# Multiplying the second block's weight pages as whole float32 instead of as high and low halves

## What is computed

```python
xn = rmsnorm(h, norm1_g)
proj = xn @ w_in                                   # 1024 -> 3584
q_a, k_a, v_a, q_r, f_r, i_r, g_r = split(proj)
attn = moba_attention(q_a, k_a, v_a)
rec = hgrn2(q_r, f_r, i_r, g_r)
h = h + concatenate([attn, rec]) @ w_out           # 1024 -> 1024
hn = rmsnorm(h, norm2_g)
h = h + peer(hn, peer_wq, peer_subkeys, peer_u, peer_v)
out = rmsnorm(h, normf_g)
```

## Time and profile before

| | us |
|---|---|
| median of three runs | 1626.68 |
| the profiled execution, its own time | 1631.37 |
| its span in the trace | 1629.6 |
| TensorE busy | 1366.6 (84%) |
| VectorE busy | 919.0 (56%) |
| ScalarE busy | 619.4 (38%) |
| GpSimd busy | 546.0 (34%) |
| start of the first of the 24 split pages of the change | about 749 |
| first expert gather | 928.76 |

### The profile page before, as it was taken

One profiled execution on the slowest core, in us unless ns is written; L12 is line 12 of the kernel. 1 busy time (PEld: TensorE's weight loads), 2 busy tenths in 40 slices (PEclk: granted clock), 3 DMA queues, 4 the chain that ended last, 5 costly groups with the idle time before them and its releaser, 6 DMA issues.

```text
span 1629.6 us, 19201 instructions
## 1 busy us (share of the span) xinstructions
PE 1366.6 (84%) x7122; PEld 994.5 (61%) x7122; DVE 919.0 (56%) x1853; ACT 619.4 (38%) x1425; POOL 546.0 (34%) x370
## 2 busy tenths in 40 slices
PE   6978959976966999999999988888777777777786
PEld 5867848955866999999878954444322322223332
DVE  2231896515353578834663646666666666666654
ACT  2002312214342566655445444334444444444443
POOL 0000000000045588887104423343443444444341
PEclk9998978968998999999999999999898889899899
DMA  5443310001334365565325499999999999999997
GB/s 200 155 130 104 104 52 1 1 0 65 104 111 135 104 190 185 181 194 166 95 79 180 166 398 389 378 387 377 396 399 404 408 406 399 400 397 402 408 403 301
DMA packets 67641, 381.03 MB, mean 234 GB/s; under 512 B 7520, under 2 KB 7648, under 8 KB 34400
## 3 DMA queue, kind: packets, MB, share of 16 engines
q0 software_dynamic: 36864, 268.45, 40.7%
q1 hardware_dynamic: 29808, 107.49, 20.6%
q10 hardware_dynamic: 880, 3.93, 0.6%
HBM read 378.79 MB, written 1.05 MB: 233 GB/s over the span
## 4 chain that ended last, share of the span: by engine, by line
PE 59%; DVE 19%; DMA 14%; ACT 4%; issue 3%; POOL 1%; DVEq 0%; SPq 0%; ACTq 0%; POOLq 0%
PE bank L397 23%; PE bank L850 15%; DMA arena_block<-in_experts,arena_block 14%; PE bank L413 4%; PE bank L425 2%; DVE arena_mix L1347 2%; PE bank L529 1%; PE bank L537 1%; PE bank L802 1%; DVE late L1828 1%; PE bank L669 1%; PE bank L535 1%; POOL arena_block L1878 1%; PE bank L395 1%; PE bank L436 1%
## 5 line engine op out<-in xcount | busy, mean ns | idle before, releaser
L850 PE MATMUL bank<-arena_block 128*128 128x512 f32 x1024 | 497.9, 638 | 140.5 <-ACT arena_block L1238 140.3
L1868 POOL TENSOR_TENSOR w_lo<-ring,w_hi 128x1024 fp32r<-128x1024 f32 x110 | 269.3, 2464 | 642.5 <-ACT w_hi L906 642.4
L850 PEld LDWEIGHTS bank<-arena_block 128*128 128x128 f32 x1024 | 201.1, 204 | 428.9 <-ACT arena_block L1238 221.6
L1828 DVE SCALAR_TENSOR_TENSOR late<-arena_block 128x1024 f32<-128x1024 f32 x256 | 307.2, 1223 | 233.0 <-DMA arena_block<-in_experts,arena_block 233.0
L1878 POOL DMA_INDIRECT arena_block<-in_experts,arena_block x256 | 276.5, 1080 | 415.3 <-PE bank L850 384.5
L1232 ACT ACTIVATE arena_block<-arena_block 128x1 f32<-128x1 f32 x256 | 51.6, 202 | 291.6 <-DVE late L1828 289.6
L906 ACT ACTIVATE w_hi<-ring 128x1024 fp32r<-128x1024 f32 x110 | 115.5, 1053 | 99.8 <-PE bank L425 37.3
L397 PE MATMUL bank<-h_norm,ring 128*128 128x256 f32 x576 | 128.3, 381 | 3.1 <-ACT arena_mix L919 3.1
L397 PEld LDWEIGHTS bank<-h_norm,ring 128*128 128x128 f32 x576 | 108.2, 190 | 20.3 <-issue 6.0
L397 PE MATMUL bank<-arena_mix,ring 128*128 128x256 f32 x480 | 107.3, 387 | 13.2 <-DMA ring<-in_pages 13.2
L397 PE MATMUL bank<-x_hi,w_hi 128*128 128x256 f32 x416 | 118.3, 284 | 0.0
(11 more groups left out here) (399 smaller groups left out, 2152.9 us busy)
## 6 DMA issues: line engine op xcount, KB each, us to landing
ring<-in_pages SPq DMA_DIRECT2D x192, 512.0 KB, 3.5
late<-in_pages SPq DMA_DIRECT2D x8, 512.0 KB
arena_block<-in_experts,arena_block POOLq DMA_INDIRECT x256, 12.5
const<-in_const ACTq DMA_DIRECT2D x1, 1136.0 KB, 9.1
x_res<-in_xT SPq DMA_DIRECT2D x2, 512.0 KB, 6.7
arena_mix<-in_memT ACTq DMA_DIRECT2D x1, 1024.0 KB, 12.8
arena_block<-in_subkT ACTq DMA_DIRECT2D x1, 1024.0 KB, 4.9
out_tok<-arena_block SPq DMA_DIRECT2D x4, 256.0 KB, 5.1
```

The lines of the kernel that those rows point to most:

```text
L850: last = mm(bank[2 * tt + j][:, :], diag[:, slot, :], uv[slot][:, D + j * 512:D + (j + 1) * 512], start=False, stop=stop)
L1828: stt(junk[r % 2], uv[s][:, 0:D], 1.0, htok[:, tt, :], ALU.mult, ALU.mult, accum_out=e_act[:, s:s + 1])\
L1868: nc.gpsimd.tensor_tensor(w_lo[:, slot, :], ring[:, slot, :], w_hi[:, slot, :].bitcast(F32), ALU.subtract)\
```

## The change

All pages from in2 on become whole. The 24 split pages are multiplied as float32 from the ring with `hn`, or with `cat` itself for out2. With them go their `w_hi` and `w_lo`, the `x_hi` and `x_lo` of the two norms of the second layer, and `cat_hi` and `cat_lo`. The ring slots of these pages now come free when TensorE has done the page. The waits of TensorE on split inputs become waits on `hn` and on `cat`.

```diff
-WHOLE = list(range(PAGE0["qk"], PAGE0["out2"])) + list(range(PLAIN0, N_PAGES))
+WHOLE = list(range(PAGE0["in2"], N_PAGES))
...
-        linear("in2", x_hi, x_lo, part=(0, 1), ready=("x_split", KT))
+        linear("in2", hn, part=(0, 1), ready=lambda k: (S("x_hn"), k + 1))
...
-            ways = [(hn, ring)] if page in WHOLE else [(x_hi, w_hi), (x_lo, w_hi), (x_hi, w_lo)]
             for k in range(KT):
-                for n_, (y, w) in enumerate(ways):
-                    last = mm(bank_of(stage, i)[:, 0:2 * P], y[:, k, tt * P:(tt + 1) * P], w[:, slot:slot + 2, k * P:(k + 1) * P],
-                              start=k == 0 and n_ == 0, stop=k == KT - 1 and n_ == len(ways) - 1)
+                last = mm(bank_of(stage, i)[:, 0:2 * P], hn[:, k, tt * P:(tt + 1) * P], ring[:, slot:slot + 2, k * P:(k + 1) * P],
+                          start=k == 0, stop=k == KT - 1)
...
-        linear("out2", cat_hi, cat_lo, ready=("cat_split", 0))
+        linear("out2", cat, ready=lambda k: (S("att_oc"), MH + 2 * k + 2) if k < 4 else (S("cat_rec"), k - 3))
...
-            if page < PLAIN0 + SLOTS:
-                ways = products(page, x_hi, x_lo)
-            else:
-                ways = [(late[:, page - PLAIN0 - SLOTS, :], hn)]
+            w = ring[:, page % SLOTS, :] if page < PLAIN0 + SLOTS else late[:, page - PLAIN0 - SLOTS, :]
...
-            A_(x_hi[:, k, :], x[:, k, :], ACT.Identity, scale=V(gain, k)).then_inc(S("x_hi"), 1)
             if i >= 3:
-                A_(hn[:, k, :], x[:, k, :], ACT.Identity, scale=V(gain, k))
+                A_(hn[:, k, :], x[:, k, :], ACT.Identity, scale=V(gain, k)).then_inc(S("x_hn"), 1)
+            else:
+                A_(x_hi[:, k, :], x[:, k, :], ACT.Identity, scale=V(gain, k)).then_inc(S("x_hi"), 1)
...
-            if h % 2:
-                act.wait_ge(S("att_oc"), MH + h + 1)
-                cat_high(ft)
...
-            norm_low(i, j, gain)
+            if i == 2:
+                norm_low(i, j, gain)
...
-            if h:
-                cat_low(3 + h)
-        cat_low(7)
```

More of the change, by code:

```diff
@@ L243, in build @@
     mg_hi, mg_lo = typed(YS_AT, ("mg_hi", "mg_lo"), KT)
-    cat_hi, cat_lo = typed(TYPED0 + 9216, ("cat_hi", "cat_lo"), KT)
     ff_space = [nc.sbuf_tensor(n, [P, FT, T], F32R) for n in ("ff_hi", "ff_lo")]
@@ L375, in products @@
             if page not in NTH:
-                return [(ring[:, slot, :], hn if page in WHOLE else hi)]
+                return [(ring[:, slot, :], hi)]
             return [(w_hi[:, slot, :], hi), (w_hi[:, slot, :], lo), (w_lo[:, slot, :], hi)]
@@ L389, in linear @@
                         if ready and b == 0:
-                            pe.wait_ge(S(ready[0]), ready[1] + k + 1)
+                            pe.wait_ge(*ready(k))
                         for n_, (w, y) in enumerate(ways):
@@ L451, in head_sum @@
             last.then_inc(S("head_sum"), 1)
-        linear("in_a", xg, part=(0, 1), ready=("xg_ready", 0))
+        linear("in_a", xg, part=(0, 1), ready=lambda k: (S("xg_ready"), k + 1))
         pe.wait_ge(S("const_in"), 16)
@@ L645, in _ @@
         linear("out", mg_hi, mg_lo)
-        linear("up", x_hi, x_lo, part=(0, 1), ready=("x_split", 0))
+        linear("up", x_hi, x_lo, part=(0, 1), ready=lambda k: (S("x_split"), k + 1))
         norm_sum(2)
@@ L649, in _ @@
         down()
-        linear("in2", x_hi, x_lo, part=(0, 1), ready=("x_split", KT))
+        linear("in2", hn, part=(0, 1), ready=lambda k: (S("x_hn"), k + 1))
         norm_sum(3)
-        linear("in2", x_hi, x_lo, part=(1, N_IN2 - 1))
+        linear("in2", hn, part=(1, N_IN2 - 1))
         pe.wait_ge(S("norm_inv"), 4)
@@ L660, in by_token @@
             page, tt = PAGE0[stage] + i - i % 2, i % 2
-            if page in WHOLE:
-                page_ready(page)
+            page_ready(page)
             page_ready(page + 1)
@@ L737, in _ @@
             if u < N_QK:
-                linear("qk", x_hi, x_lo, part=(u, 1))
+                linear("qk", hn, part=(u, 1))
             elif u < N_QK + N_TI:
@@ L741, in _ @@
             else:
-                linear("g2", x_hi, x_lo, part=(u - N_QK - N_TI, 1))
+                linear("g2", hn, part=(u - N_QK - N_TI, 1))
             if u == 0:
@@ L793, in query @@
                 pe.wait_ge(S("wq_out"), b - 1)
-            if page < PLAIN0 + SLOTS:
-                ways = products(page, x_hi, x_lo)
-            else:
-                ways = [(late[:, page - PLAIN0 - SLOTS, :], hn)]
+            w = ring[:, page % SLOTS, :] if page < PLAIN0 + SLOTS else late[:, page - PLAIN0 - SLOTS, :]
             for k in range(KT):
                 if b == 0:
[L800 to L803, removed]
+                    pe.wait_ge(S("x_hn"), KT + k + 1)
+                last = mm(bank[4 + b % 2][:, 0:T], w[:, k * P:(k + 1) * P], hn[:, k, :], start=k == 0, stop=k == KT - 1)
             last.then_inc(S("page_done"), 1)
@@ L1080, in _ @@
                 norm_tile(3, "down", j, "norm1_g_2")
-        high_ahead(PAGE0["in2"])
         norm_root(3)
         for b in range(1, N_IN2):
-            high_ahead(PAGE0["in2"] + b)
             if b == 4:
@@ L1127, in mb_done @@
             A_(cat[o:o + 64, ft, :], bank[6 + h % 2][o:o + 64, 0:T], ACT.Copy).then_inc(S("att_oc"), 1)
-            if h % 2:
-                act.wait_ge(S("att_oc"), MH + h + 1)
-                cat_high(ft)
-        def cat_high(k):
-            A_(cat_hi[:, k, :], cat[:, k, :], ACT.Copy).then_inc(S("cat_hi"), 1)
         take_rtok(0, 5)
         act.wait_ge(S("rtok_in"), 1)
-        high_ahead(PAGE0["tv"])
         act.wait_ge(S("in2_out"), N_IN2)
@@ L1197, in _ @@
                 A_(hg_in, hg_in, ACT.Silu).then_inc(S("h_act"), 1)
-        for h in range(GH):
-            act.wait_ge(S("cat_rec"), h + 1)
-            cat_high(4 + h)
         for j in range(KT):
-            high_ahead(PAGE0["out2"] + j)
             if j:
@@ L1683, in mb_share @@
             ts(p_[:, P:3 * P], p_[:, P:3 * P], r_[:, 1:2], None, ALU.mult).then_inc(S("att_p"), 1)
-        def cat_low(k):
-            dve.wait_ge(S("cat_hi"), k + 1)
-            tt_(cat_lo[:, k, :], cat[:, k, :], cat_hi[:, k, :].bitcast(F32), ALU.subtract).then_inc(S("cat_split"), 1)
         for b in range(4):
```

7 lines of the change are left out of this document (removed).

## The result

| | before | after |
|---|---|---|
| median, 11 runs each, on one chip | 1628.68 us | 1637.15 us |
| lowest and highest | 1625.85, 1633.5 | 1635.02, 1640.11 |
| ratio | | 1.0050 (95%: 1.0038 to 1.0062) |

The change makes the kernel slower by 0.5%, some 8.5 us (6.2 to 10.1 by the interval). The profiled execution took 1640.11 us, the longest of the eleven.

The account below looks back on a forecast made before the run. TensorE was taken to bound the kernel up to the first expert gather, transfers from there on. 10.7 us to head 0's scores, -0.85 for the clock and +2.5 for late pages gave 12.3 us: 1639.0 us, range 1634.5 to 1643.

Parts of the forecast that it names:

- The price of a page: On TensorE, a whole page takes 3.46 us against 2.88 split, 0.58 us more; 24 pages make 13.9 us.
- the four passes of the Trainium skill: Rival: a whole page costs four passes at the split price, 3.84 us, 9 us above the sum; chance 0.01.
- in2 and tv: Twelve pages turned whole cost 7.0 us, less stalls of 0.23 and 0.34 us that go: +6.4 us.
- qk to g2: Pages already whole, with no one on the chain waiting for the removed copies and subtractions: 0, bounds -0.5 to +0.5.
- The ring: Page slots are held until TensorE is through, yet loads land in time: 0, upper bound about 2 us at one place.
- out2 and its clock: Out2 pages +3.4 us; the low clock behind the idle time costs 0 or -1.7, half taken: -0.85.
- Queries 0 and 1: First two query pages: +0.35 us for query 0, 0.58 for query 1 with its clock loss kept; +0.9 us.
- The late pages: Loads issued near the first gather come later and move the fourth dot product and the end: +2.5 us, bounds 0 and 3.5.
- The ScalarE wait of 11.4 us: Expert stage's start; rival of failed feeding lets it grow or ring loads come late: 3 to 8 us more, chance 0.07.
- The signs of being wrong: Wrong if a stretch without changed pages changes its length by over 1 us, or TensorE waits for a ring load.
- the 938 to 940: Time in us at which the first expert gather was expected to start in the changed kernel.
- The rival "absorbed": Expert stage's seams take in 2 us or more of delay, leaving +3.3 to +7.8 us, 1630 to 1634.5; chance 0.07.

Follow-up runs that it names:

- e_out2wq: Out2 and the first four query pages whole, in2 and tv split as in the kernel before; 1.0040 of before.
- e_all_early: The changed kernel with the late pages and the last norm's weights loaded between the ring loads of qk to g2; 1.0026 of before.
- e_wq_late: Only the first four query pages whole, with the late pages and last norm's weights loaded once out2 is done; 0.9978 of before.
- before_third: The unchanged kernel before, executed for a third trace; 696.59 us from the first gather to the end.
- after_again: The changed kernel, run once more against the kernel before; 1.0062 of before.
- e_wq_only: Only the first four query pages whole; in2, tv and out2 split as in the kernel before; 1.0012 of before.
- e_wq_late_warm: e_wq_late plus five matmuls of unused result in TensorE's idle time ahead of out2's fifth block; 0.9970 of before.
- e_order_late: e_wq_late_warm with queries 6 and 7 and head 3's scores moved on TensorE to between the expert stage's first four rows; 0.9993 of before.

## Why the prediction was right, and where not

The direction, the range (1634.5 to 1643) and the order of the terms held: 1637.15 us against 1639.0. The size was 12.3 us and came out as 8.5, 3.8 less; the median stood closer than that by luck, because the kernel before came out at 1628.68 in eleven runs, 2.0 us above the three that I had.

- **The price of a page, right.** 3.46 us at every whole page. The measured ratio to a split page is 1.20; with the four passes of the Trainium skill (FP8 and Floating Point Precision, TensorE Precision Notes) at the price of a split product each, it would be 1.33, and the 24 pages 9 us dearer. No row supports that price.
- **in2 and tv: +6.4 predicted, +6.10 measured** in three traces. The 0.3 us between them is mostly that the split pages cost a little more than 2.88 us each: seven in2 pages took 20.34 us in before and 24.18 in after, the four tv pages 12.26 and 13.92. The scans, beside which no GpSimd subtraction runs any more, are short, and TensorE doesn't wait for their bank. The Trainium skill's rule on the shared port (SBUF — State Buffer, Who interferes with whom) fits: 666 to 681 ns now, 659 to 2882 before. From the trace of after, ns least/median/most:
```profile
L1672 DVE TENSOR_TENSOR_SCAN arena_block<-const,arena_block x4: 666/668/681, 777.1 to 778.9; 128x256 f32<-128x256 f32 x4
```
- **qk to g2: 0 and 0.00. The ring: 0.** No ring load delayed TensorE in the chain of after; loads of 740 to 960 landed in 3.4 to 5.0 us, in 3.4 to 6.3 before.
- **out2 and its clock: +3.4 - 0.85 = +2.55 predicted, +1.93 measured.** What was weak here is the half: the loss stays or goes, and half of it is a value that cannot come out. With the clock up the whole sum would have been 1.7 (measured 1.93 in three traces), with it down 3.4 (measured 3.62 in e_out2wq). Both branches were right to 0.25 us; only which of them comes was open, and no run shows what decides it. For the split pages of before, the 1.7 us as a loss that a warm clock gives back was over-read: 0.65 to 0.98 came back. For the whole pages it was right: 1.69.
- **Queries 0 and 1: +0.9 predicted, +1.12 measured,** with 1.67 more where the clock stays down through query 1. The prediction took that loss as fixed and it is not.
- **The late pages: +2.5 predicted, +0.4 in the mean of the traces. This is the step that failed.** The delay is real: late loads 1.56 us later against the first gather, 8th dot 2.4 us later. That it moves the end in full is the inference that fell, by the intervals above rather than by the traces, whose scatter is wider than the term. I had said that from the first gather on a fixed volume passes at a fixed rate; e_all_early and e_wq_late show that it doesn't, for 4.7 MB less brought 4 to 6 us where the rate gives 11.8. I also placed the delay at the fourth dot, and it came at the eighth.
- **The ScalarE wait of 11.4 us**, which a rival rested on, is not in after, and not in before_third either, so it comes and goes without the change.
- **The signs of being wrong.** One of them fired: two stretches without changed pages moved by over 1 us, +3.32 down to in2 and -3.75 in the expert stage. Both lie within what happens without the change: in2 starts between 748.0 and 752.9 us over all traces, and the expert stage of before differs by 5.3 us from one to the next. The sign was set too fine. The first gather came at 941.21 us in after, past the 938 to 940, and at 939.87 in after_again.
- **A slip in a rival.** Free late pages, a clock that stays up and seams that take in 2 us or more leave at most 10.7 - 1.7 - 2 = 7.0 us, not 7.8. It changes nothing in the forecast.

In sum, 9.8 us predicted up to the first gather, 9.13 and 10.80 measured; 2.5 behind it, 0.4 in the mean. The rest, to 8.5, lies within the interval. The rival "absorbed" had the more fitting picture behind the first gather, but its seams took in about 2 us, not the 4 to 8 that its time needed.

Nothing in the change makes the kernel faster: each of its parts that was run by itself was slower than before or equal to it. The kernel with the lowest time here keeps in2, tv and out2 split, makes only the four query pages whole, loads the late pages early and fills TensorE's gap ahead of out2: 1623.88 us, 0.9970 of before. Early loads with the query pages still split were not run; e_wq_only against before suggests that whole query pages only cost.

## What to carry to other kernels

Price a changed operation from the same operation elsewhere in the trace, then ask stage by stage whether that engine ends the stage: that gave two of the three terms up to the gathers to 0.3 us and the third, with its clock, to 0.6. Do not turn a full-looking DMA share into "every byte costs its time": here it stood at 0.97, and of a delay of 2.4 us no more than 0.4 showed in the mean end, and 4.7 MB taken away brought less than half of their time. When a wait stands out in a trace, try moving it before calling it the limit: the first refill was moved forward by 4 and 9 us, and the 16th gather did not come earlier. Where a cost is one of two values, forecast one of them and give the other a chance; before calling a difference an effect, cut two traces of the same kernel at the same events and see which stages repeat.

## What was unexpected in the hardware

- The same idle time of TensorE, 2.04 us at the same point of the program, was followed by a granted clock of 1.00 in three traces and of 0.50 in one; with 1.10 us the clock stayed at 1.00 in both traces of it (e_wq_late_warm, e_order_late).
- Behind the first eight gathers the late loads delay the eighth gather's rows by 2.4 us and the fourth's by nothing. That fits transfers of two queues being served side by side; no run tries it by itself.
- The expert stage of one kernel differs by up to 5.3 us from one execution to the next, while the stages between in2 and it repeat to 0.3 us within one kernel, the one at query 1 apart.
- The granted clock fell to 0.50 at query 1 in the traces of before and of after though TensorE's records fill the norm's sum ahead of it, 2.00 us of every 2 us.
